# Relaid weights for a two-layer hybrid decoder step: each 1 MB slot read as 128 rows of 8 KB instead of 2 KB (and 4 KB) rows

## The chip, the cores and the metric

The kernel runs on one core of one Trainium2 chip. The metric is the device time of one execution in microseconds. Three runs of the kernel before took 2315.47, 2316.97 and 2317.2 us; the median is 2316.97 us. Host work (laying out arrays before the launch) is outside the metric.

## What is computed

The reference is one inference step of a decoder trunk with two layers, for 256 prompt tokens and 8 sequences of 8 tokens (320 tokens of width 1024, float32). Cut to the order of the work:

```python
for layer in range(2):
    mod = silu(c) @ w_ada[layer] + b_ada[layer]        # 1024 x 6144: six vectors of shift, scale and gate
    h = rmsnorm(x) * (1 + sc_m) + sh_m
    if layer == 0:
        out, states = mixer_ab(h)                      # h @ ab_w_in (1024 x 4104), delta rule + HGRN2, @ ab_w_out (1024 x 1024)
    else:
        out, states = mixer_ssd(h)                     # h @ ssd_w_in (1024 x 5152), SSD scan, @ ssd_w_out (2048 x 1024)
    x = x + g_m * out
    h = rmsnorm(x) * (1 + sc_f) + sh_f
    x = x + g_f * moe(h)                               # 16 experts, top 2 of one group; gate, up 1024 x 512, down 512 x 1024
y = rmsnorm(x)
```

All weights together are some 300 MB and each is read once from HBM in an execution.

## The kernel before

One core holds all 320 tokens in SBUF, with features on the 128 partitions. The weights stream through a ring of eight **slots** (`SLOTS = 8`), each 128 partitions x 2048 float32, that is 1 MB or 8 KB per partition. `load` (line 361) fills the next slot: SP waits until TensorE has counted `weights_used` far enough, then issues one DMA. TensorE takes slots in the same order with `next_slot` (line 561) and gives them back through `weights_used`.

What SP issues stands in program order and sets the order of the transfers: `load_cond` for blocks of `w_ada` (two slots for 512 columns), `load_square` for a matrix in blocks of 512 columns (one slot is 512 rows, so four rows of 2 KB per partition), and `experts` for the mixture of experts (MoE): per expert two slots each of gate, up (2 KB rows) and down (two rows of 4 KB per partition). The slot's source is a rearranged view of the weight as the caller gave it:

```python
wk = w.rearrange("(k p) n -> p k n", p=P)
for c0 in cols:
    for k0 in range(0, nk, 4):
        load(wk[:, k0:k0 + 4, c0:c0 + BANK])
```

At the start SP issues the conditioning vector `cs` (from `c_t`), two slots of `w_ada`, the tables `const` and `small`, then six slots more, `x`, and three small tails (`router`, `ab_tail`, `dt_tail`). TensorE's first wait is for `const` and `small` (line 1047).

In the MoE of each layer the tokens go through HBM. GpSimd scatters token rows of 4 KB into `x_rows` by ten indirect DMAs (line 490); SP loads 128 rows per expert from there (`tokens`, line 400); ACT stores each expert's result into `y_rows` (line 1315, 512 KB in rows of 4 KB); when all have landed, GpSimd gathers two rows per token from `y_rows` by ten indirect DMAs (line 497), and VectorE adds them into `x`. SP goes on meanwhile: after the last expert come the `w_ada` slots of `COND_BACK` and the next layer's first weights. These loads go out as TensorE frees slots.

The two output projections (`projections`, line 579) take all slots of a group of 512 columns before their first matmul: two for layer 0, four for `ssd_w_out` of layer 1. SP issues them after `mixer_done`.

DMAs go out on three queues: SP's (all weight loads and the `x_rows` loads), ACT's (the `y_rows` stores) and GpSimd's (the states in and out, the scatter, the gather and the final `y`). `y` is stored as 1024 rows of 320 values (line 537).

Of the kernel before, what the change touches and what calls it, by code (L numbers as in the profile page):

```python
# [25 lines left out]
P = 128  # L26
D = 1024
DK = D // P
PROMPT = 256
SEQS, SEQ_LEN = 8, 8  # L30
T = PROMPT + SEQS * SEQ_LEN
# [3 lines left out]
MODS = 1 + SEQS  # L35
TAPS = 4
PAD = TAPS - 1
# [4 lines left out]
HEADS = 4  # L42
BLOCKS = HEADS * CHUNKS
AB_CONV = 12
AB_TAIL = 2 * HEADS
AB_TAIL_AT = 2048

SX = 16
SG = 4
SHPG = 8  # L50
SH = SG * SHPG
SXBC = 24
SSD_IN = 5152
# [6 lines left out]
SLOT = 2048  # L60
SLOTS = 8
BANKS = 4
BANK = 512
# [6 lines left out]
COND_MIXED = ([(0, 8), (0, 9)], [(1, 8), (1, 9)])  # L70
# [72 lines left out]
def trunk_program(nc, a, out):  # L143
    with ExitStack() as ctx:
        def sb(name, cols, parts=P):
            return ctx.enter_context(nc.sbuf_tensor(name, [parts, cols], F32))

        def sem(name):
            return ctx.enter_context(nc.semaphore(name))
# [4 lines left out]
        x = sb("x", DK * T)  # L154
        h = sb("h", DK * T)
        cs = sb("cs", DK * MODS)
        mod0 = sb("mod0", 48 * MODS)
        router = sb("router", DK * E)
        ab_tail = sb("ab_tail", DK * AB_TAIL)
        dt_tail = sb("dt_tail", DK * SH)  # L160
# [34 lines left out]
        def slot(n):  # L195
            at = RING + (n % SLOTS) * SLOT
            return pool[:, at:at + SLOT]
# [40 lines left out]
        k = Plan((0, ab_free), (ab_lo_end, pool_cols))  # L238
# [52 lines left out]
        o = Plan((0, MOD1_AT - 2100))  # L291
# [9 lines left out]
        cond_in = sem("cond_in")  # L301
        x_in = sem("x_in")
        tails_in = sem("tails_in")
# [5 lines left out]
        weights_in = [sem(f"weights_in{i}") for i in range(SLOTS)]  # L309
# [37 lines left out]
        left_weights_in = by_layer("left_weights_in")  # L347
# [10 lines left out]
        @block.sync  # L358
        def _(sp):
            n = Count()  # L360

            def load(src):

                i = n.n.get(id(weights_used), 0)
                if i >= SLOTS:
                    sp.wait_ge(weights_used, n.at(weights_used, 1 - SLOTS))
                n.up(weights_used)
                sp.dma_start(slot(i).rearrange("p (k n) -> p k n", n=src.shape[-1]), src) \
                    .then_inc(weights_in[i % SLOTS], 16)

            def load_cond(groups):
                for layer, g_ in groups:
                    load_square(a["w_ada"][layer], [g_ * BANK], DK)

            def load_square(w, cols, nk):

                wk = w.rearrange("(k p) n -> p k n", p=P)
                for c0 in cols:
                    for k0 in range(0, nk, 4):
                        load(wk[:, k0:k0 + 4, c0:c0 + BANK])  # L380

            def experts(layer):
                wg, wu, wd = a["moe_w_gate"][layer], a["moe_w_up"][layer], a["moe_w_down"][layer]

                def gate_up(e):
                    for w in (wg, wu):
                        wk = w[bass.ds(e, 1)].rearrange("o (k p) n -> p (o k) n", p=P)
                        for k0 in (0, 4):
                            load(wk[:, k0:k0 + 4, :])

                def down(e):
                    wk = wd[bass.ds(e, 1)].rearrange("o (k p) n -> p (o k) n", p=P)
                    for k0 in (0, 2):
                        load(wk[:, k0:k0 + 2, :])

                def tokens(e, b, reuse=True):
                    if reuse:
                        n.up(xe_turned)
                        sp.wait_ge(xe_turned, n.at(xe_turned))
                    sp.dma_start(XE[b], x_rows[bass.ds(e * CAP, CAP), :]).then_inc(xe_in[b], 16)  # L400

                load_cond(COND_AGAIN[layer] + COND_ROUTE[layer] + COND_MOVE[layer])
                gate_up(0)
                sp.wait_ge(scattered, 16 * 2 * CHUNKS * (layer + 1))
                tokens(0, 0, False)
                tokens(1, 1, False)
                gate_up(1)
                down(0)
                with sp.Fori(0, TURNS) as i:
                    with n.repeat(i, TURNS, {weights_used: 6 * EXPERTS_A_TURN, xe_turned: EXPERTS_A_TURN}):  # L410
                        for j in range(EXPERTS_A_TURN):
                            e = i * EXPERTS_A_TURN + (2 + j)
                            tokens(e, j % 2)
                            gate_up(e)
                            down(i * EXPERTS_A_TURN + (1 + j))
                for e in range(2 + TURNS * EXPERTS_A_TURN, E):
                    tokens(e, e % 2)
                    gate_up(e)
                    down(e - 1)
                down(E - 1)  # L420
                n.up(xe_turned, 2)
                load_cond(COND_BACK[layer])
                sp.wait_ge(overflow_known, layer + 1)
                with sp.If(sp.value_load(overflow[0:1, layer:layer + 1], min_val=0, max_val=1) > 0):
                    with sp.Fori(0, E) as e:

                        sp.wait_ge(left_weights_free[layer], e + 1)
                        for i, w in enumerate((wg, wg, wu, wu, wd, wd)):
                            wk = w[bass.ds(e, 1)].rearrange("o (k p) n -> p (o k) n", p=P)
                            nk = wk.shape[1] // 2  # L430
                            sp.dma_start(slot(i).rearrange("p (k n) -> p k n", k=nk), wk[:, i % 2 * nk:(i % 2 + 1) * nk, :]) \
                                .then_inc(left_weights_in[layer], 16)
                    sp.wait_ge(left_weights_free[layer], E + 1)

            sp.dma_start(cs[:, :].rearrange("p (k n) -> p k n", k=DK), a["c_t"].rearrange("(k p) n -> p k n", p=P)).then_inc(cond_in, 16)
            load_cond(COND_FIRST[0][:1])
            for dst, src in ((const, a["consts"]), (small, a["small"])):
                sp.dma_start(dst[:, :], src).then_inc(consts_in, 16)
            load_cond(COND_FIRST[0][1:])
            sp.dma_start(x[:, :].rearrange("p (k n) -> p k n", k=DK), a["x_t"].rearrange("(k p) n -> p k n", p=P)).then_inc(x_in, 16)  # L440
            for dst, src, k_ in ((router, a["router_w"], DK), (ab_tail, a["ab_w_in"][0][:, AB_TAIL_AT:AB_TAIL_AT + AB_TAIL], DK),
                                 (dt_tail, a["ssd_w_in"][0][:, SSD_IN - SH:SSD_IN], DK)):
                sp.dma_start(dst[:, :].rearrange("p (k n) -> p k n", k=k_), src.rearrange("(k p) n -> p k n", p=P)).then_inc(tails_in, 16)
            load_cond(COND_NORM[0])
            load_square(a["ab_w_in"][0], [0, 512, 1024, 1536] + [AB_TAIL_AT + AB_TAIL + BANK * i for i in range(4)], DK)
            for layer, w_out, nk in ((0, a["ab_w_out"][0], DK), (1, a["ssd_w_out"][0], SX)):
                if layer == 1:
                    load_cond(COND_NORM[1])
                    load_square(a["ssd_w_in"][0], [BANK * i for i in range(4, 10)] + [BANK * i for i in range(4)], DK)

                sp.wait_ge(ring_opens, layer + 1)
                if layer == 0:
                    load_cond(COND_MIXED[0][:1])
                    load_square(a["w_ada"][0][0:BANK], [COND_MIXED[0][1][1] * BANK], DK // 2)
                    sp.wait_ge(mixer_done, 1)
                    load_square(a["w_ada"][0][BANK:D], [COND_MIXED[0][1][1] * BANK], DK // 2)
                else:
                    load_cond(COND_MIXED[1])
                    sp.wait_ge(mixer_done, 2)
                load_square(w_out, (0, BANK), nk)  # L460
                experts(layer)


# [1 line left out]
        def _(pool_eng):  # L465
            n = Count()

            def store(dst, src):

                pool_eng.wait_ge(out_ready, n.up(out_ready))  # L470
                n.up(stored, 16)
                pool_eng.dma_start(dst, src).then_inc(stored, 16)
# [61 lines left out]
                               SSS[q % 2].rearrange("p (b n) -> p b n", b=SEQS)).then_inc(stored_state[q % 2], 16)  # L534
            store(out["ssd_p"], ST)
            exchange(1)
            store(out["y"].rearrange("(k p) n -> p k n", p=P), h[:, :].rearrange("p (k n) -> p k n", k=DK))
            pool_eng.wait_ge(stored, n.at(stored))
            for i in range(2):
                pool_eng.wait_ge(stored_state[i], 16 * SG // 2)  # L540
# [1493 lines left out]

_WEIGHTS = ("w_ada", "ab_w_in", "ab_w_out", "ssd_w_in", "ssd_w_out", "moe_w_gate", "moe_w_up", "moe_w_down")


def _constants():  # L2040
# [100 lines left out]
```

## Time and profile before

| | |
|---|---|
| median of 3 runs | 2316.97 us (2315.47 to 2317.2) |
| profiled execution, span from first to last instruction | 2319.4 us (no other time is given for it) |
| PE busy | 1974.0 us, 85% |
| DVE, ACT, POOL busy | 600.3, 302.9, 53.9 us |
| mean granted TensorE clock | 0.827 |
| SP's queue (weights, x_rows) | 145776 packets, 321.13 MB |
| GpSimd's queue | 11632 packets, 50.98 MB |
| ACT's queue (y_rows stores) | 4608 packets, 16.78 MB |

The profile is of one execution on the chip; its times are microseconds from the first instruction. PE stands for TensorE's matmuls, PEld for its weight loads, DVE for VectorE, ACT for ScalarE, POOL for GpSimd, and a name with q (SPq, POOLq) for that engine's instruction queue. L944 is line 944 of the kernel. DMA transfers are read from the issue to the landing, and from the stretches of time in which the profile gives the gigabytes per second and the busy share of the 16 DMA engines (overlapping packets can take it a little over 1).

### The profile page before, as it was taken

To read this page: it belongs to the slowest core of one execution; us is meant where nothing else is said; L and a number is where in the kernel's file an instruction comes from. 1 tells how busy PE (TensorE), PEld (TensorE's weight loads), DVE (VectorE), ACT (ScalarE), POOL (GpSimd) and SP (SyncE) were. 2 spreads that over 40 slices of the span, in tenths; PEclk is the share of its full clock that TensorE was granted. 3 is DMA by queue.
4 is the path that set the end of the run, shared out by engine and by line. 5 is a ranking of instruction groups with operands and counts; after the bars stand their busy time and mean duration, and the time that the engine had idled before them with its cause. 6 is when DMAs were issued, how large, how long until landed. Compare 5 with 4: busy or idle time off the path is not lost.

```text
span 2319.4 us, 19065 instructions
## 1 busy us (share of the span) xinstructions
PE 1974.0 (85%) x7290; PEld 1146.4 (49%) x7290; DVE 600.3 (26%) x1226; ACT 302.9 (13%) x538; POOL 53.9 (2%) x68
## 2 busy tenths in 40 slices
PE   7999578758889999999689989999979599999972
PEld 2566378757453444444246655556636344444431
DVE  0230533374230000000234214575620300000004
ACT  1121201021011111111012210110000111111110
POOL 0000000000001000000100000000000100000001
PEclk9999655565889999999889985555589799999995
DMA  9880100010838888888823220220074188888842
GB/s 333 244 244 1 45 1 1 5 73 5 290 109 298 291 301 309 289 311 291 245 87 132 79 69 4 73 73 36 15 257 145 56 310 308 287 308 298 296 151 56
DMA packets 162097, 390.01 MB, mean 168 GB/s; under 512 B 10848, under 2 KB 12000, under 8 KB 161376
## 3 DMA queue, kind: packets, MB, share of 16 engines
q1 hardware_dynamic: 145776, 321.13, 40.7%
q0 software_dynamic: 11632, 50.98, 6.4%
q10 hardware_dynamic: 4608, 16.78, 1.8%
q8 instruction: 56, 0.92, 0.2%
q14 instruction: 25, 0.20, 0.0%
HBM read 339.87 MB, written 48.99 MB: 168 GB/s over the span
## 4 chain that ended last, share of the span: by engine, by line
PE 77%; DVE 9%; issue 6%; ACT 3%; DMA 3%; POOL 1%; DVEq 0%; SPq 0%; ACTq 0%; POOLq 0%
PE bank L944 29%; PE bank L587 18%; PE bank L657 5%; PE bank L612 4%; PE bank L892 2%; PE bank L897 2%; PE bank L868 2%; PE bank L887 1%; PE bank L636 1%; PE bank L730 1%; PE bank L884 1%; PE bank L628 1%; PE bank L697 1%; PE bank L936 1%; ACT pool L1296 1%
## 5 line engine op out<-in xcount | busy, mean ns | idle before, releaser
L944 PE MATMUL bank<-pool 128*128 128x512 f32 x1536 | 684.1, 598 | 35.1 <-PE bank L944 12.3
L944 PEld LDWEIGHTS bank<-pool 128*128 128x128 f32 x1536 | 285.6, 191 | 391.9 <-issue 385.8
L587 PE MATMUL bank<-h,pool 128*128 128x320 f32 x1280 | 354.2, 438 | 5.2 <-PE bank L587 5.2
L587 PEld LDWEIGHTS bank<-h,pool 128*128 128x128 f32 x1280 | 244.4, 192 | 113.6 <-issue 16.7
L612 PE MATMUL bank<-pool,cs 128*9 128x512 f32 x384 | 175.9, 612 | 14.3 <-DMA small<-small_in 12.0
L1935 DVE COPY pool<-bank 128x512 f32<-128x512 f32 x32 | 22.1, 691 | 506.1 <-PE bank L966 506.1
L657 PE MATMUL bank<-pool 64*64 64x64 f32 (+2 forms) x920 | 118.0, 327 | 22.2 <-DVE pool L1582 16.9
L657 PEld LDWEIGHTS bank<-pool 64*64 64x64 f32 (+2 forms) x920 | 114.7, 238 | 27.6 <-DVE pool L1582 18.3
L612 PEld LDWEIGHTS bank<-pool,cs 128*9 128x9 f32 x384 | 33.9, 93 | 145.1 <-issue 132.5
L1941 DVE TENSOR_TENSOR pool<-bank,pool 128x512 f32<-128x512 f32 x32 | 22.1, 691 | 244.7 <-PE bank L944 244.7
L587 PE MATMUL bank<-pool 128*128 128x320 f32 x256 | 71.3, 441 | 8.0 <-DMA pool<-ssd_w_out_in 7.6
L1296 ACT ACTIVATE pool<-bank 128x512 f32<-128x512 f32 x64 | 34.8, 594 | 274.1 <-PE bank L936 274.1
L892 PEld LDWEIGHTS bank<-pool 128*128 128x128 f32 x256 | 55.8, 330 | 23.7 <-issue 23.7
L1313 ACT ACTIVATE pool<-bank 128x512 f32<-128x512 f32 x64 | 38.2, 597 | 220.2 <-PE bank L944 220.2
L936 PE MATMUL bank<-const,pool 128*128 128x128 f32 x256 | 35.1, 281 | 35.5 <-DMA pool<-x_rows 25.2
L587 PEld LDWEIGHTS bank<-pool 128*128 128x128 f32 x256 | 49.5, 194 | 29.3 <-issue 9.9
L1465 DVE SCALAR_TENSOR_TENSOR pool<-pool,small 128x344 f32<-128x344 f32 x108 | 62.3, 576 | 3.8
L936 PEld LDWEIGHTS bank<-const,pool 128*128 128x128 f32 x256 | 28.1, 143 | 59.8 <-issue 34.4
L892 PE MATMUL bank<-pool 128*128 128x8 f32 x256 | 57.3, 362 | 0.0
L897 PE MATMUL bank<-pool 64*128 64x512 f32 x64 | 56.1, 1067 | 0.0
L628 PE MATMUL bank<-h,const 128*128 128x320 f32 x80 | 31.2, 559 | 27.3 <-ACT h L1098 25.2
L1303 ACT ACTIVATE pool<-bank 128x512 f32<-128x512 f32 x32 | 19.1, 598 | 230.9 <-PE bank L944 230.9
(334 smaller groups left out, 1526.7 us busy)
## 6 DMA issues: line engine op xcount, KB each, us to landing
pool<-moe_w_gate_in SPq DMA_DIRECT2D x64, 1024.0 KB, 7.7
pool<-moe_w_up_in SPq DMA_DIRECT2D x64, 1024.0 KB, 7.0
pool<-moe_w_down_in SPq DMA_DIRECT2D x64, 1024.0 KB, 5.1
pool<-w_ada_in SPq DMA_DIRECT2D x48, 1024.0 KB, 8.7
pool<-ssd_w_in_in SPq DMA_DIRECT2D x20, 1024.0 KB, 5.6
pool<-ab_w_in_in SPq DMA_DIRECT2D x16, 1024.0 KB, 12.1
pool<-x_rows SPq DMA_DIRECT2D x32, 512.0 KB, 5.7
y_rows<-pool ACTq DMA_DIRECT2D x32, 512.0 KB, 7.3
```

The source lines that it names most:

```text
L587: mm = pe.matmul(b[:, 0:T], ws[kk // 4][:, kk % 4, mt * P:(mt + 1) * P], rhs[:, kk * T:(kk + 1) * T], start=(kk == 0), stop=(kk == nk - 1))
L612: mm = pe.matmul(b[0:MODS, :], cs[:, (k0 + kk) * MODS:(k0 + kk + 1) * MODS], w[:, kk, :], start=(k0 + kk == 0), stop=(k0 + kk == DK - 1))
L628: mm = pe.matmul(b[:, 0:T], ones, h[:, kk * T:(kk + 1) * T], start=(kk == 0), stop=(kk == DK - 1))
L657: mm = pe.matmul(b[0:parts, (i - i0) * width:(i - i0 + 1) * width], lhs(i), rhs(i), start=True, stop=True)
L868: pe.matmul(b[0:C, 0:T], SEL[:, (gi * SHPG + hh) * C:(gi * SHPG + hh + 1) * C], G, start=True, stop=True).then_inc(dve_full, 1)
L892: mm = pe.matmul(reads[:, o:o + SEQ_LEN], states[:, s_ * BANK + j * P:s_ * BANK + (j + 1) * P], Cf[:, PROMPT + s_ * SEQ_LEN:PROMPT + (s_ + ...
L897: pe.matmul(b[:, :], BM[:, s_ * P:(s_ + 1) * P], XEND[:, PC * BANK:CHUNKS * BANK], start=True, stop=True).then_inc(dve_full, 1)
L936: mm = pe.transpose(b[:, (kk - k0) * P:(kk - k0 + 1) * P], XE[q][:, kk * P:(kk + 1) * P], ident)
L944: mm = pe.matmul(b[:, :], lhs[:, kk * CAP:(kk + 1) * CAP], ws[kk // per][:, kk % per, col:col + BANK], start=(kk == 0), stop=(kk == nk - 1))
L1296: act.activation(XT[q][:, i * BANK:(i + 1) * BANK], b[:, :], ACT.Copy).then_inc(act_free, 1)
L1313: act.activation(YE[q][:, i * BANK:(i + 1) * BANK], b[:, :], ACT.Copy).then_inc(act_free, 1)
L1465: ins = stt(cv, up[:, j:j + CVW], w[:, f * TAPS + j:f * TAPS + j + 1], cv, ALU.mult, ALU.add)
```

## The change

The host lays every large weight out in the order in which the slots are taken, so that the slot's bytes in HBM are 128 rows of 8 KB, one row per partition. `x`, `c`, `router`, the two tails and the output `y` are laid out by partition as well (`x` and `y` in rows of 10 KB). The bytes are the same, and no instruction of any engine is added, dropped or moved; each DMA keeps its place in its queue and loses its inner dimension.

```diff
-                sp.dma_start(slot(i).rearrange("p (k n) -> p k n", n=src.shape[-1]), src) \
-                    .then_inc(weights_in[i % SLOTS], 16)
+                sp.dma_start(slot(i), src).then_inc(weights_in[i % SLOTS], 16)
...
-                    load_square(a["w_ada"][layer], [g_ * BANK], DK)
+                    load_blocks(a["w_ada"][layer, g_])
...
+            def load_blocks(w):
+
+                for j in range(w.shape[0]):
+                    load(w[j])
...
+                def half(w, e, j):
+                    return w[bass.ds(e * 2 + j, 1)].rearrange("o p n -> (o p) n")
+
                 def gate_up(e):
                     for w in (wg, wu):
-                        wk = w[bass.ds(e, 1)].rearrange("o (k p) n -> p (o k) n", p=P)
-                        for k0 in (0, 4):
-                            load(wk[:, k0:k0 + 4, :])
+                        for j in range(2):
+                            load(half(w, e, j))
...
-            sp.dma_start(cs[:, :].rearrange("p (k n) -> p k n", k=DK), a["c_t"].rearrange("(k p) n -> p k n", p=P)).then_inc(cond_in, 16)
+            sp.dma_start(cs[:, :], a["c_t"]).then_inc(cond_in, 16)
...
-            store(out["y"].rearrange("(k p) n -> p k n", p=P), h[:, :].rearrange("p (k n) -> p k n", k=DK))
+            store(out["y"], h[:, :])
...
+def _rows(w):
+
+    w = np.asarray(w)
+    return w.reshape(-1, P, w.shape[-1]).transpose(1, 0, 2).reshape(P, -1)
...
+def _blocks(w, cols):
+
+    w = np.asarray(w)
+    return np.stack([w[:, c:c + BANK].reshape(-1, 4, P, BANK).transpose(0, 2, 1, 3).reshape(-1, P, SLOT) for c in cols])
...
+def _expert_halves(w):
+
+    layers, experts, rows, cols = w.shape
+    return w.reshape(layers, experts * 2, rows // (2 * P), P, cols).transpose(0, 1, 3, 2, 4).reshape(layers, experts * 2, P, SLOT)
```

The start of SP's program, before (the shape at a row's end is partitions x rows per partition x elements):

```order
L435 DMA cs<-c_t_in 128x8x9
L368 DMA pool<-w_ada_in 128x4x512 x2
L438 DMA const<-consts_in 128x1059
L438 DMA small<-small_in 128x438
L368 DMA pool<-w_ada_in 128x4x512 x6
L440 DMA x<-x_t_in 128x8x320
```

And the same place in the changed kernel:

```order
L435 DMA cs<-c_t_in 128x72
L368 DMA pool<-w_ada_in 128x2048 x2
L438 DMA const<-consts_in 128x1059
L438 DMA small<-small_in 128x438
L368 DMA pool<-w_ada_in 128x2048 x6
L440 DMA x<-x_t_in 128x2560
```

The order is the same; a slot's transfer has 128 rows where it had 512, `cs` has 128 rows of 288 bytes where it had 1024 of 36, and `const` and `small` are as they were.

## Rows read from the trace of the kernel before

**Rows 1.** The page: span, and TensorE's busy time, share and instructions.

```profile
span 2319.4 us, 19065 instructions
PE 1974.0 (85%) x7290; PEld 1146.4 (49%) x7290; DVE 600.3 (26%) x1226; ACT 302.9 (13%) x538; POOL 53.9 (2%) x68
```

**Rows 2.** Busy us by engine, PEclk, DMA share, GB/s: first MoE; last expert's end.

```profile
720.00:1105.00 385.00, 358.41 (x936) 158.77 (x936) 21.63 (x32) 45.39 (x78) 0.00 (x0) 1.00 0.85 301
...
2248.00:2252.00 4.00, 4.00 (x10) 1.52 (x8) 0.00 (x0) 0.60 (x1) 0.00 (x0) 1.00 0.00 0
```

**Rows 3.** Chain that ended last (start, us, what): one product mid-MoE, the last one.

```profile
885.90 7.12 PE bank L944 x16
...
2245.05 7.12 PE bank L944 x16
```

**Rows 4.** Waits for DMAs: total us, times, longest us.

```profile
PE bank L936 <- DMA pool<-x_rows: 25.2, 2, 23.9
...
PE bank L612 <- DMA small<-small_in: 12.0, 1, 12.0
...
PE bank L587 <- DMA pool<-ssd_w_out_in: 7.6, 1, 7.6
...
DVE pool L1962 <- DMA pool<-y_rows,pool: 35.7, 2, 27.1
```

**Rows 5.** Same columns as Rows 2: w_ada slots, 2 KB rows; gdn_state, 16 KB rows.

```profile
18.00:30.00 12.00, 11.70 (x31) 2.49 (x30) 0.20 (x1) 1.17 (x2) 0.00 (x0) 1.00 1.05 388
240.00:244.00 4.00, 0.88 (x8) 0.79 (x8) 2.83 (x9) 0.74 (x2) 0.00 (x0) 0.50 1.06 446
```

**Rows 6.** Timeline: first matmuls (start, us); columns of Rows 2: the stretch before.

```profile
11.99 9.55 PE L612 MATMUL bank<-pool,cs 128*9 128x512 f32 x16 [11.99 <-DMA small<-small_in]
...
3.50:12.00 8.50, 0.01 (x1) 0.01 (x1) 0.00 (x0) 0.21 (x1) 0.00 (x0) 1.00 1.03 385
```

**Rows 7.** DMA issues: KB each, median us from issue to landing.

```profile
y_out<-h POOLq DMA_DIRECT2D x1, 1280.0 KB, 5.3
ssd_p_out<-pool POOLq DMA_DIRECT2D x1, 1024.0 KB, 4.2
...
cs<-c_t_in SPq DMA_DIRECT2D x1, 36.0 KB, 2.7
```

**Rows 8.** Chain that ended last, before layer 1's output projection.

```profile
1704.47 11.80 DMA pool<-ssd_w_out_in
```

**Rows 9.** First scatter's last DMA (chain), and TensorE's wait behind it (timeline).

```profile
709.06 6.19 DMA x_rows<-pool
...
718.56 1.09 PE L936 MATMUL bank<-const,pool 128*128 128x128 f32 x8 [1.36 <-DMA pool<-x_rows]
```

**Rows 10.** Chain: last y_rows store and last gather of layer 0; last store, layer 1.

```profile
1113.57 7.39 DMA y_rows<-pool
...
1132.57 12.61 DMA pool<-y_rows,pool
...
2252.82 2.63 DMA y_rows<-pool
```

**Rows 11.** Columns of Rows 2: gather with loads, loads left over, gather alone.

```profile
1127.00:1144.00 17.00, 8.70 (x30) 2.33 (x28) 0.82 (x4) 1.18 (x2) 4.93 (x6) 0.88 1.04 243
...
1145.00:1150.50 5.50, 2.04 (x16) 1.86 (x16) 4.90 (x6) 0.00 (x0) 0.00 (x0) 0.50 1.03 382
...
2259.00:2270.00 11.00, 0.00 (x0) 0.00 (x0) 0.00 (x0) 0.00 (x0) 6.79 (x8) 0.50 0.92 207
```

**Rows 12.** hgrn_s_out's store (timeline; DMA issues), and its stretch beside w_ada loads.

```profile
580.53 0.53 POOL L472 DMA_DIRECT2D hgrn_s_out<-pool  x1 [19.59 <-DVEq L1393]
...
hgrn_s_out<-pool POOLq DMA_DIRECT2D x1, 2048.0 KB, 11.6
...
582.00:592.00 10.00, 6.67 (x34) 5.39 (x33) 2.51 (x4) 3.08 (x3) 0.00 (x0) 0.50 0.96 357
```

**Rows 13.** DMA issue (KB, us to landing) of the ssd_w_in slot issued at 1127.69.

```profile
pool<-ssd_w_in_in SPq DMA_DIRECT2D x1, 1024.0 KB, 18.8
```

More of the change, by code:

```diff
@@ L367, in load, with load_matrix @@
                 n.up(weights_used)
-                sp.dma_start(slot(i).rearrange("p (k n) -> p k n", n=src.shape[-1]), src) \
-                    .then_inc(weights_in[i % SLOTS], 16)
+                sp.dma_start(slot(i), src).then_inc(weights_in[i % SLOTS], 16)
             def load_cond(groups):
                 for layer, g_ in groups:
-                    load_square(a["w_ada"][layer], [g_ * BANK], DK)
[L375 to L380, printed above, removed]
+                    load_blocks(a["w_ada"][layer, g_])
+            def load_blocks(w):
+                for j in range(w.shape[0]):
+                    load(w[j])
+            def load_matrix(w):
+                for g_ in range(w.shape[0]):
+                    load_blocks(w[g_])
             def experts(layer):
                 wg, wu, wd = a["moe_w_gate"][layer], a["moe_w_up"][layer], a["moe_w_down"][layer]
+                def half(w, e, j):
+                    return w[bass.ds(e * 2 + j, 1)].rearrange("o p n -> (o p) n")
                 def gate_up(e):
                     for w in (wg, wu):
-                        wk = w[bass.ds(e, 1)].rearrange("o (k p) n -> p (o k) n", p=P)
-                        for k0 in (0, 4):
-                            load(wk[:, k0:k0 + 4, :])
+                        for j in range(2):
+                            load(half(w, e, j))
                 def down(e):
-                    wk = wd[bass.ds(e, 1)].rearrange("o (k p) n -> p (o k) n", p=P)
-                    for k0 in (0, 2):
-                        load(wk[:, k0:k0 + 2, :])
+                    for j in range(2):
+                        load(half(wd, e, j))
                 def tokens(e, b, reuse=True):
@@ L428, in experts @@
                         for i, w in enumerate((wg, wg, wu, wu, wd, wd)):
[L429 to L432, printed above, removed]
+                            sp.dma_start(slot(i), half(w, e, i % 2)).then_inc(left_weights_in[layer], 16)
                     sp.wait_ge(left_weights_free[layer], E + 1)
-            sp.dma_start(cs[:, :].rearrange("p (k n) -> p k n", k=DK), a["c_t"].rearrange("(k p) n -> p k n", p=P)).then_inc(cond_in, 16)
+            sp.dma_start(cs[:, :], a["c_t"]).then_inc(cond_in, 16)
             load_cond(COND_FIRST[0][:1])
@@ L439, in _ @@
             load_cond(COND_FIRST[0][1:])
[L440 to L443, printed above, removed]
+            sp.dma_start(x[:, :], a["x_t"]).then_inc(x_in, 16)
+            for dst, src in ((router, a["router_w"]), (ab_tail, a["ab_tail"]), (dt_tail, a["dt_tail"])):
+                sp.dma_start(dst[:, :], src).then_inc(tails_in, 16)
             load_cond(COND_NORM[0])
-            load_square(a["ab_w_in"][0], [0, 512, 1024, 1536] + [AB_TAIL_AT + AB_TAIL + BANK * i for i in range(4)], DK)
-            for layer, w_out, nk in ((0, a["ab_w_out"][0], DK), (1, a["ssd_w_out"][0], SX)):
+            load_matrix(a["ab_w_in"])
+            for layer, w_out in ((0, a["ab_w_out"]), (1, a["ssd_w_out"])):
                 if layer == 1:
                     load_cond(COND_NORM[1])
-                    load_square(a["ssd_w_in"][0], [BANK * i for i in range(4, 10)] + [BANK * i for i in range(4)], DK)
+                    load_matrix(a["ssd_w_in"])
                 sp.wait_ge(ring_opens, layer + 1)
@@ L453, in _ @@
                     load_cond(COND_MIXED[0][:1])
-                    load_square(a["w_ada"][0][0:BANK], [COND_MIXED[0][1][1] * BANK], DK // 2)
+                    last = a["w_ada"][0, COND_MIXED[0][1][1]]
+                    load(last[0])
                     sp.wait_ge(mixer_done, 1)
-                    load_square(a["w_ada"][0][BANK:D], [COND_MIXED[0][1][1] * BANK], DK // 2)
+                    load(last[1])
                 else:
@@ L459, in _ @@
                     sp.wait_ge(mixer_done, 2)
-                load_square(w_out, (0, BANK), nk)
+                load_matrix(w_out)
                 experts(layer)
@@ L2033, in _ @@
             normalise(None)
-_WEIGHTS = ("w_ada", "ab_w_in", "ab_w_out", "ssd_w_in", "ssd_w_out", "moe_w_gate", "moe_w_up", "moe_w_down")
+def _rows(w):
[7 more added lines that the diff above has]
+    return w.reshape(layers, experts * 2, rows // (2 * P), P, cols).transpose(0, 1, 3, 2, 4).reshape(layers, experts * 2, P, SLOT)
 def _constants():
@@ L2108 @@
         "consts": consts, "levels": levels, "small": _small(v),
-        "x_t": np.concatenate([v["x_prompt"].reshape(-1, D), v["x_sample"].reshape(-1, D)]).T,
-        "c_t": np.concatenate([v["c_prompt"], v["c_sample"]]).T,
-        "router_w": v["router_w"],
+        "x_t": _rows(np.concatenate([v["x_prompt"].reshape(-1, D), v["x_sample"].reshape(-1, D)]).T),
+        "c_t": _rows(np.concatenate([v["c_prompt"], v["c_sample"]]).T),
+        "router_w": _rows(v["router_w"]),
+        "ab_tail": _rows(v["ab_w_in"][0][:, AB_TAIL_AT:AB_TAIL_AT + AB_TAIL]),
+        "dt_tail": _rows(v["ssd_w_in"][0][:, SSD_IN - SH:SSD_IN]),
+        "w_ada": np.stack([_blocks(w, range(0, 6 * D, BANK)) for w in v["w_ada"]]),
+        "ab_w_in": _blocks(v["ab_w_in"][0], [BANK * i for i in range(4)] + [AB_TAIL_AT + AB_TAIL + BANK * i for i in range(4)]),
+        "ab_w_out": _blocks(v["ab_w_out"][0], (0, BANK)),
+        "ssd_w_in": _blocks(v["ssd_w_in"][0], [BANK * i for i in range(4, 10)] + [BANK * i for i in range(4)]),
+        "ssd_w_out": _blocks(v["ssd_w_out"][0], (0, BANK)),
+        "moe_w_gate": _expert_halves(v["moe_w_gate"]), "moe_w_up": _expert_halves(v["moe_w_up"]),
+        "moe_w_down": _expert_halves(v["moe_w_down"]),
         "gdn_conv_t": conv_t(v["state_gdn_conv"]), "ssd_conv_t": conv_t(v["state_ssd_conv"]),
@@ L2116 @@
     }
-    arrays |= {name: v[name] for name in _WEIGHTS}
     arrays = {name: np.ascontiguousarray(x) for name, x in arrays.items()}
-    shapes = {"y": (D, T), "gdn_p": (P, HEADS * P), "gdn_s": (P, SEQS * HEADS * P), "gdn_conv": (P, AB_CONV * MODS * PAD),
+    shapes = {"y": (P, DK * T), "gdn_p": (P, HEADS * P), "gdn_s": (P, SEQS * HEADS * P), "gdn_conv": (P, AB_CONV * MODS * PAD),
               "hgrn_p": (P, HEADS * P), "hgrn_s": (P, SEQS * HEADS * P), "ssd_p": (P, SH * C), "ssd_s": (P, SEQS, SH * C),
@@ L2132, in conv_out @@
         return m[:, 0:1], m[:, 1:]
-    y = r["y"].T
+    y = r["y"].reshape(P, DK, T).transpose(1, 0, 2).reshape(D, T).T
     gc, sc_ = conv_out(r["gdn_conv"]), conv_out(r["ssd_conv"])
```

## The prediction, made before the changed kernel ran

> **What bounds the kernel now.** Begin with the engines' busy times: TensorE is busy for 1974.0 of 2319.4 us, 85% [rows 1]. That is an average, so the stages come next. In the first MoE the matmuls take 358.41 of 385 us, at the full clock, while the DMA engines are busy for 0.85 of the time and move 301 GB/s [rows 2]. This is the stage with by far the most loads (192 of the 288 slots, six for each of 32 experts in both layers together), and its transfers hide behind TensorE. They do not slow the matmuls either: a product of 16 matmuls takes 7.12 us in the middle of it and 7.12 us at its end [rows 3], where almost nothing moves any more [rows 2]. So faster loads are worth nothing for two thirds of the slots.
>
> What can be gained stands in the waits for DMAs [rows 4]. TensorE waits 12.0 us at the start for `small`; 7.6 us for `ssd_w_out`; 25.2 us in two pieces for `x_rows`, of which 23.9 us lie in layer 1, where the scatter before it has no weight load beside it; and VectorE waits 35.7 us in two pieces for the gather from `y_rows`, 27.1 us of it at the end of layer 1, again with no weight load beside it. All other waits of TensorE are for other engines. The change therefore acts at five places: the start, the first scatter, the layer-0 gather, `ssd_w_out`, and the final store.
>
> **The price of a slot.** With 2 KB rows and a full queue the loads move 388 GB/s [rows 5], so a slot of 1.049 MB takes 2.70 us. No load of the trace has 8 KB rows. The nearest rows are the 16 KB rows of `gdn_state`: 446 GB/s over 4 us [rows 5], 2.35 us for a slot's bytes. Per engine of 16, a 2 KB row then costs 84.5 ns and a 16 KB row 588 ns, which a fixed 12.5 ns and 36.0 ns per KB fit; 8 KB would be 300 ns, or 2.40 us a slot. The 4 us stretch is short, so I take **2.45 us, 0.25 us saved per slot**, with 0 and 0.35 as ends.
>
> The Trainium skill, page "DMA: Bandwidth & Descriptors", section "Specifications", gives 512 bytes as the smallest transfer for line rate; by that, 2 KB rows are at line rate already, and the slots save nothing. The two stretches (388 against 446 GB/s) speak against it; what it would give is the second rival below.
>
> **The change part by part.** No instruction moves and no wait is added; the sum has these terms.
>
> 1. *Start.* `small` lands at 11.99 us, behind `cs` and two slots, on a queue that is full from 3.5 us on (385 GB/s) [rows 6]. Two slots save 0.5 us. `cs` took 2.7 us to land for 36 KB [rows 7]; before 3.5 us its 1024 short rows hold the queue. 128 rows instead save between 0 and 1 us; I take 0.4, nearer to 0, because most of 2.7 us is what any transfer takes (the last `y_rows` store, 512 KB, landed in 2.63 us [rows 10]). **-0.9** (ends 0 and -1.7). TensorE runs on without a DMA wait until the scatter, so this passes to the end. The larger early loads (`x`, the tails) become faster at no gain: TensorE is busy meanwhile.
>
> 2. *First scatter.* It runs beside two slots of the up weights, its last DMA takes 6.19 us, and TensorE waits 1.36 us for the load behind it [rows 9]. Two slots save 0.5 us of DMA time, of which I count **-0.3** (0 to -1.36, all that there is to gain).
>
> 3. *Layer-0 store and gather.* The last `y_rows` store takes 7.39 us where the undisturbed one of layer 1 takes 2.63, and the last gather 12.61 us [rows 10], because TensorE frees slots in these 30 us and SP refills them. Gather and loads together move only 243 GB/s with all DMA engines busy; the gather alone moves 207; after its end the loads go on at 382 GB/s for 5.5 us [rows 11]. So when the gather ended, 2.1 MB, two slots, were still to come. If long rows let the loads take a larger share, those two could at worst all run ahead of it: 2 x 2.45 = +4.9 us, less 4 x 0.25 for the slots that run ahead anyway: +3.9. At best the gather moves as if alone: its 2.62 MB (ten DMAs of 64 rows of 4 KB) at 207 GB/s take 12.7 us instead of 17: -4.3. Which end is nearer? The trace has one place where long rows meet short ones. `hgrn_s_out` is stored in 16 KB rows beside `w_ada` loads of 2 KB; it was issued at 580.53 and landed 11.6 us later, and from 582 to 592 us 3.57 MB moved in all [rows 12]. The store is 2.10 MB, so the loads got 1.47 MB, 0.70 byte per byte of the store, though their rows were an eighth as long. In the gather's 17 us, 4.13 MB moved, 1.51 of it loads: 0.58 per byte, with rows half as long. The share hardly follows the row length. I take a little of the bad end, **+0.7**.
>
> 4. *`ssd_w_out`.* Four slots are issued in a row and TensorE starts when the fourth lands, 11.80 us after its issue [rows 8]; the wait is 7.6 us [rows 4]. Four slots save **-1.0** (0 to -1.4). The other four are needed a whole projection group later and are hidden.
>
> 5. *Final store.* `y` (1280 KB in 1024 rows) lands in 5.3 us; `ssd_p_out`, 1024 KB in 8 KB rows, in 4.2 [rows 7]. A quarter MB more at 446 GB/s adds 0.6, so 4.8: **-0.5** (0 to -1.0).
>
> Elsewhere the loads have cover: the MoE's by the matmuls (0.15 of the DMA time free), the input projections' by TensorE's own pace, since no wait for them is listed. Cost 0 for these; if the cover went, see the last rival.
>
> Sum: -0.9 - 0.3 + 0.7 - 1.0 - 0.5 = **-2.0 us**, 0.09%. The profiled execution's span is 2.4 us above the median of the runs, 2316.97; I apply the difference to the median: **2315.0 us**. About 0.2%, 4.6 us, is what a measurement of this kernel can tell from no change, so the forecast is no difference.
>
> **Rivals.**
>
> *Long rows win over the gather (slower).* If an engine takes one row from each queue in turn, 8 KB of load goes for each 4 KB row of the gather and of the last store, the loads run first, and the gather lands up to 3.9 us later; with half of the other gains (-1.35) the kernel ends 2.5 us later: 2319.5. It decides from the point where the loads get more than about one byte per byte of the gather. For it: a slot issued in that stretch needs 18.8 us to land now [rows 13], so the loads are held back. Against it: the 0.70 above; strict turns would have left the loads 0.13. The Trainium skill, page "DMA: Bandwidth & Descriptors", section "Queues, rings and completion order", says that each engine goes round its queues packet by packet; by that rule this rival is the result. The stretch at 582 us does not bear it out in its strict form.
>
> *No gain in rate.* The slots stay at 2.70 us; what is left is `cs` and the final store, -0.9: 2316.1.
>
> *The gather is freed (faster).* If fewer, longer rows stop holding up the gather's, term 3 becomes -4.3, and the sum -7.0: 2310.0. For it: 243 GB/s with all engines busy is far under 388, so the mixture itself is what is slow. Against it: nothing shows that the number of rows is the cause, since the gather alone reaches only 207.
>
> *8 KB rows are slow (much slower).* An expert takes some 24.1 us (385 us for 16) and leaves 0.15 of DMA time free [rows 2], 0.60 us for each of its six slots. Above 3.3 us a slot (317 GB/s) the MoE waits for its weights; at 300 GB/s, 3.5 us, that is 0.2 x 192 = 38 us: 2355. Against it: 446 GB/s with 16 KB rows.
>
> **How the numbers follow.** Forecast 0.52, long rows win 0.20, no gain in rate 0.10, gather freed 0.13, slow rows 0.05. Faster by over 0.2% takes the freed gather and the forecast's best edge (0.08, where terms 1, 2, 4 and 5 near their best ends, -5.5): 0.21. Slower takes the slow rows, and 0.06 for long rows winning with none of the gains and the store late as well: 0.11. The rest, 0.68, is within. The range goes from the freed gather, 2310, to the long rows with none of the other gains (+3.9), 2320.9; it leaves out the slow rows and the tails.
>
> **What would show it.** In the changed profile: full-queue stretches of weight loads near 425 GB/s (right) or 388 (wrong); `small` landing near 11.1; the wait for `ssd_w_out` near 6.6 us; `y` landing in 4.8; SP's packets down by about 100,000; MoE products still 7.12 us. Term 3 is judged by the gather's last landing, counted from the last expert's store: now 31.6 us (1113.57 to 1145.18). Clearly more, and the long rows win; near 27, and it is freed. A MoE with waits for weights would make the prediction wrong altogether.

## The result and the profile after

The changed kernel takes **2324.14 us** (median of 12 runs, 2317.69 to 2329.88). The kernel before, timed beside it on the same chip, takes 2317.52 (12 runs, 2315.47 to 2321.93). The ratio is 1.0025, 95% interval 1.0013 to 1.0036: slower by 3.0 to 8.3 us, where 2 us faster was forecast; the median also lies above the upper end of the forecast range, 2320.9. The profiled execution of the change took 2329.88 us, its slowest run, with a span of 2328.1, 8.7 above the span of [rows 1].

First the page and the stretches that answer to [rows 1, 2, 5, 6]. Columns of the windows: stretch, length, busy us of PE, PEld, DVE, ACT and POOL, PEclk, DMA share, GB/s.

```profile
span 2328.1 us, 19065 instructions
PE 1971.3 (85%) x7290; PEld 1142.6 (49%) x7290; DVE 600.4 (26%) x1226; ACT 303.2 (13%) x538; POOL 53.6 (2%) x68
...
q1 hardware_dynamic: 47088, 321.13, 37.6%
```

```profile
18.00:30.00 12.00, 11.70 (x32) 2.46 (x30) 0.19 (x1) 1.17 (x2) 0.00 (x0) 1.00 1.02 415
3.50:12.00 8.50, 0.80 (x1) 0.11 (x2) 0.00 (x0) 0.00 (x0) 0.00 (x0) 1.00 1.02 417
720.00:1105.00 385.00, 358.85 (x935) 158.79 (x933) 21.42 (x31) 45.36 (x78) 0.00 (x0) 0.99 0.82 300
```

SP's queue (q1: packets, MB, share) moves the same 321.13 MB in 47088 packets; before it needed 145776. A full queue of loads runs at 415 to 417 GB/s where it ran at 385 to 388, so a slot takes 2.5 us and not 2.7. In the MoE the DMA share falls from 0.85 to 0.82, the rate stays, and TensorE's busy time is what it was: the faster loads buy nothing there.

Now the chain that ended last (start, us, what), the rows that answer to [rows 3, 8 to 10], and VectorE's and TensorE's waits (total us, times, longest) that answer to [rows 4].

```profile
708.10 7.44 DMA x_rows<-pool
...
1107.36 7.12 PE bank L944 x16
1115.13 7.61 DMA y_rows<-pool
1134.36 20.72 DMA pool<-y_rows,pool
1177.39 7.53 PE bank L628 x16
...
1200.35 4.78 PE bank L636 x80
1205.13 17.44 PE bank L587 x64
1222.86 17.48 PE bank L587 x64
...
1712.85 11.01 DMA pool<-ssd_w_out_in
```

```profile
DVE pool L1962 <- DMA pool<-y_rows,pool: 44.0, 2, 27.1
...
PE bank L936 <- DMA pool<-x_rows: 26.7, 2, 24.2
...
PE bank L587 <- DMA pool<-ssd_w_out_in: 6.5, 1, 6.5
```

The start, the first scatter's wait and the final store, that answer to [rows 6, 9, 7], in the timeline and in the DMA issues (KB each, us to landing):

```profile
11.20 1.02 PE L612 MATMUL bank<-pool,cs 128*9 128x512 f32 x1 [11.20 <-DMA small<-small_in]
...
718.85 1.70 PE L936 MATMUL bank<-const,pool 128*128 128x128 f32 x8 [2.57 <-DMA pool<-x_rows]
```

```profile
y_out<-h POOLq DMA_DIRECT2D x1, 1280.0 KB, 4.7
...
cs<-c_t_in SPq DMA_DIRECT2D x1, 36.0 KB, 1.8
```

Three of the five places became faster: `small` lands at 11.20 (11.99 before), `ssd_w_out` takes 11.01 us (11.80), `y` lands in 4.7 (5.3). The main loss stands in one row: the last gather of layer 0 takes 20.72 us where it took 12.61. From the issue of the last expert's store to the end of the gather it is now 1115.13 to 1155.08, **39.95 us, 8.35 more than before**. The store's own row hardly changes (7.39 to 7.61 us). VectorE's wait grows by the same 8.3, 35.7 to 44.0, and all of it in layer 0: the longest piece, layer 1's, is still 27.1.

What did the loads do in that time? The view of the DMA queues shows it. Each row is a queue with its packets, MB and share of 16 engines; q1 carries the loads, q0 the gather. First the kernel before from 1130 to 1144 us, then the change from 1130 to 1150.

```profile
q0 software_dynamic: 637, 2.10, 61.4%
q1 hardware_dynamic: 716, 1.43, 42.6%
```

```profile
q1 hardware_dynamic: 504, 3.74, 69.5%
q0 software_dynamic: 515, 1.68, 31.9%
```

Count rows, not bytes. (A queue's packets include some under 512 bytes, so the rows are counted from the megabytes.) Before, 2.10 MB of 4 KB gather rows are 513 rows, and 1.43 MB of 2 KB load rows are 698: 1.36 load rows for each gather row, 0.68 byte per byte. After, 1.68 MB are 410 gather rows and 3.74 MB are 456 load rows of 8 KB: 1.11 rows for each, but **2.2 bytes per byte**. The number of load rows that slip in between two gather rows hardly changed; each of them is four times as long. A gather row now comes every 0.78 us on each engine (20 us over 410/16 rows), before every 0.44 us (14 us over 513/16).

The loads run ahead of the gather, and at its end none is left:

```profile
1135.00:1154.00 19.00, 2.56 (x13) 0.82 (x10) 0.39 (x2) 0.59 (x1) 0.26 (x1) 0.61 0.94 252
1154.00:1158.00 4.00, 0.73 (x7) 0.73 (x8) 2.71 (x3) 0.00 (x0) 0.00 (x0) 0.50 0.00 0
```

Before, 5.5 us of loads at 382 GB/s followed the gather [rows 11], beside work that didn't need them. The same bytes now stand in front of it: from the last store's issue to the gather's end the loads' queue moved 6.06 MB before (1113.57 to 1145.18 us) and 8.06 MB in the change (1115.13 to 1155.08), two slots more.

```profile
q1 hardware_dynamic: 3049, 6.06, 63.2%
...
q1 hardware_dynamic: 1112, 8.06, 64.9%
```

### The profile page after: what moved, and what is told of

Its sections match the earlier page's. It is cut to its first block, busy times and chain, and to the rows that moved or that the text cites. A ratio compares the mean times of both kernels' runs of the same rounds, so it can differ in the third digit from the quotient of the medians.

```text
span 2328.1 us, 19065 instructions
## 1 busy us (share of the span) xinstructions
PE 1971.3 (85%) x7290; PEld 1142.6 (49%) x7290; DVE 600.4 (26%) x1226; ACT 303.2 (13%) x538; POOL 53.6 (2%) x68
## 3 DMA queue, kind: packets, MB, share of 16 engines
q1 hardware_dynamic: 47088, 321.13, 37.6%
## 4 chain that ended last, share of the span: by engine, by line
PE 77%; DVE 9%; issue 6%; DMA 3%; ACT 3%; POOL 1%; DVEq 0%; SPq 0%; ACTq 0%; POOLq 0%
PE bank L944 29%; PE bank L587 18%; PE bank L657 5%; PE bank L612 4%; PE bank L892 2%; PE bank L897 2%; PE bank L868 2%; PE bank L887 1%; PE bank L884 1%; PE bank L730 1%; PE bank L636 1%; PE bank L628 1%; PE bank L936 1%; PE bank L697 1%; DMA pool<-y_rows,pool 1%
## 5 line engine op out<-in xcount | busy, mean ns | idle before, releaser
L587 PE MATMUL bank<-h,pool 128*128 128x320 f32 x1280 | 351.3, 435 | 5.3 <-PE bank L587 5.3
L587 PEld LDWEIGHTS bank<-h,pool 128*128 128x128 f32 x1280 | 242.7, 191 | 112.6 <-issue 14.9
L612 PE MATMUL bank<-pool,cs 128*9 128x512 f32 x384 | 175.7, 612 | 13.5 <-DMA small<-small_in 11.2
L587 PE MATMUL bank<-pool 128*128 128x320 f32 x256 | 72.1, 445 | 6.9 <-DMA pool<-ssd_w_out_in 6.5
L1296 ACT ACTIVATE pool<-bank 128x512 f32<-128x512 f32 x64 | 34.9, 594 | 275.8 <-PE bank L936 275.8
L936 PE MATMUL bank<-const,pool 128*128 128x128 f32 x256 | 35.7, 285 | 37.0 <-DMA pool<-x_rows 26.7
L1313 ACT ACTIVATE pool<-bank 128x512 f32<-128x512 f32 x64 | 38.2, 597 | 220.4 <-PE bank L944 220.4
L587 PEld LDWEIGHTS bank<-pool 128*128 128x128 f32 x256 | 50.0, 196 | 28.6 <-issue 9.4
L1007 PE MATMUL bank<-const,pool 64*128 64x64 f32 x80 | 11.1, 317 | 51.7 <-DVEq L1393 47.7
```

Of the source, the lines that this page charges most:

```text
L587: mm = pe.matmul(b[:, 0:T], ws[kk // 4][:, kk % 4, mt * P:(mt + 1) * P], rhs[:, kk * T:(kk + 1) * T], start=(kk == 0), stop=(kk == nk - 1))
L612: mm = pe.matmul(b[0:MODS, :], cs[:, (k0 + kk) * MODS:(k0 + kk + 1) * MODS], w[:, kk, :], start=(k0 + kk == 0), stop=(k0 + kk == DK - 1))
L936: mm = pe.transpose(b[:, (kk - k0) * P:(kk - k0 + 1) * P], XE[q][:, kk * P:(kk + 1) * P], ident)
L1296: act.activation(XT[q][:, i * BANK:(i + 1) * BANK], b[:, :], ACT.Copy).then_inc(act_free, 1)
L1313: act.activation(YE[q][:, i * BANK:(i + 1) * BANK], b[:, :], ACT.Copy).then_inc(act_free, 1)
```

## The experiments

Two theories. **Turns**: at the gather each DMA engine gives the two queues about equally many rows in turn, so the length of the load rows sets the gather's pace. **Another cause**: a loss in some other place (first scatter, MoE), or one that comes from the weights being contiguous in HBM and not from the rows.

### Rows of 2 KB only at the gather

The changed kernel; the 24 slots that SP issues around the gather (four of `w_ada`, twenty of `ssd_w_in`) are still each one contiguous piece of HBM, but are read in 2 KB rows.

```diff
-                    load_cond(COND_NORM[1])
-                    load_matrix(a["ssd_w_in"])
+                    for g_ in range(2):
+                        load_short(a["w_ada_norm1"][g_])
+                    for g_ in range(10):
+                        load_short(a["ssd_w_in"][g_])
...
+    return np.stack([w[:, c:c + BANK].reshape(-1, 4, P, BANK) for c in cols])
```

> The changed kernel, with the 4 w_ada slots and the 20 ssd_w_in slots that SP issues around layer 0's gather laid out so that a slot is one piece of 1 MB in HBM but is read in rows of 2 KB. Theory (row length): gather as in the kernel before, last DMA about 12.6 us (20.7 in the changed kernel), time about 2 us under the kernel before, 2315 to 2317. Rival (that the slot is one piece of HBM, or anything else of the new layout, is the cause): 2322 to 2326, the gather's last DMA near 20 us.

Measured: 2315.40 us (11 runs) beside 2316.09 for the kernel before (20 runs), ratio 0.9994, 0.9983 to 1.0005. The chain of this kernel:

```profile
1112.97 7.10 DMA y_rows<-pool
1131.71 12.19 DMA pool<-y_rows,pool
```

The gather is back at 12.19 us, with contiguous weights. So the row length did it. What is left of the change is -3.9 to +1.2 us, which holds the -2.7 that the prediction's terms give without its third, but zero as well.

### Rows of 8 KB only at the gather

The converse: the kernel before, with only those 24 slots in 8 KB rows.

```diff
-                    load_cond(COND_NORM[1])
-                    load_square(a["ssd_w_in"][0], [BANK * i for i in range(4, 10)] + [BANK * i for i in range(4)], DK)
+                    for w in [a["w_ada_norm1"][g_] for g_ in range(2)] + [a["ssd_w_in_long"][g_] for g_ in range(10)]:
+                        for j in range(2):
+                            load(w[j])
```

> The kernel before, with only those 24 slots in rows of 8 KB. Theory: the gather's last DMA near 20 us, time 5 to 9 us above the kernel before, 2322 to 2327. Rival (the loss is elsewhere, as at the first scatter): within 2 us of the kernel before.

Measured: 2326.25 us (5 runs) beside the same 2316.09, ratio 1.0039, 1.0026 to 1.0053: **6 to 12 us slower**. Its chain:

```profile
1113.47 8.45 DMA y_rows<-pool
1133.54 19.49 DMA pool<-y_rows,pool
```

These 24 slots alone bring the whole loss, and none of the gains. The queues from 1130 to 1150 us:

```profile
q1 hardware_dynamic: 478, 3.41, 63.2%
q0 software_dynamic: 587, 1.93, 38.4%
```

That is 416 load rows of 8 KB and 471 gather rows, 0.88 for each.

### Rows of 4 KB at the gather

The changed kernel with the same 24 slots in 4 KB rows, as long as the gather's own.

```diff
-    return np.stack([w[:, c:c + BANK].reshape(-1, 4, P, BANK) for c in cols])
+    return np.stack([w[:, c:c + BANK].reshape(-1, 2, 2, P, BANK).transpose(0, 1, 3, 2, 4).reshape(-1, 2, P, 2 * BANK) for c in cols])
```

> The changed kernel, with the 24 slots around layer 0's gather in rows of 4 KB (2 KB gave a last gather DMA of 12.2 us and 2315.4 us, 8 KB 20.7 and 2324.1). Theory (each DMA engine takes one row from the loads and one from the gather in turn): rows as long as the gather's give the loads about one byte per byte of the gather; last gather DMA near 16 us, time between the two, 2318 to 2321. Rival (the engines share by bytes, and only rows past some length do harm): as with 2 KB, last DMA under 13.5 us, 2314 to 2317.

Measured: 2321.48 us (12 runs) beside 2317.02 (18 runs), ratio 1.0013, 1.0004 to 1.0022. Its chain, and its queues from 1124 to 1146 us:

```profile
1112.17 5.81 DMA y_rows<-pool
1129.59 18.27 DMA pool<-y_rows,pool
```

```profile
q1 hardware_dynamic: 720, 2.77, 55.7%
q0 software_dynamic: 713, 2.34, 47.9%
```

2.77 MB are 676 load rows, 2.34 MB are 571 gather rows: 1.18 for each. From the last store's issue to the end of the gather it is 35.7 us, between the 31.6 and 39.95 of the two kernels. The order came out as forecast, with the gather longer (18.27 us for 16) and the time 0.5 us above the forecast's 2318 to 2321; the rival of that run, a last gather under 13.5 us, is out. The dose follows the length of the rows:

| load rows | load rows per gather row | bytes per byte | one gather row per engine | last gather DMA |
|---|---|---|---|---|
| none (8 KB rows with the wait, below) | 0 | 0 | 0.32 us | 4.9 us |
| 2 KB (before) | 1.36 | 0.68 | 0.44 us | 12.61 us |
| 2 KB only at the gather | 1.45 | 0.73 | 0.46 us | 12.19 us |
| 4 KB | 1.18 | 1.2 | 0.62 us | 18.27 us |
| 8 KB only at the gather | 0.88 | 1.8 | 0.68 us | 19.49 us |
| 8 KB (the change) | 1.11 | 2.2 | 0.78 us | 20.72 us |

Each row is counted in a stretch of 12 to 22 us of that kernel's gather (1128 to 1143 us for the third, with 1.54 MB of loads and 2.12 MB of gather). By the second and fourth columns a load row of 2 KB adds (0.44 - 0.32)/1.36 = 0.09 us to a gather row, one of 8 KB (0.78 - 0.32)/1.11 = 0.41, and (0.68 - 0.32)/0.88 = 0.41 where only the 24 slots have such rows. Alone on a full queue they take 0.084 us at 388 GB/s and 0.32 at 415. So a gather row pays at least the full price of every load row that goes in between.

### The loads wait for the gather

In both kernels, SP waits for the gather before it issues those 24 slots. The `w_ada` slots of `COND_BACK` stay ahead of the wait.

```diff
                 if layer == 1:
+                    sp.wait_ge(gathered, 16 * 2 * CHUNKS)
                     load_cond(COND_NORM[1])
```

With 8 KB rows:

> The changed kernel (8 KB rows everywhere), but SP waits for layer 0's gather to land before it issues the next layer's first loads (4 slots of w_ada, then ssd_w_in). Theory (8 KB rows of loads beside the gather hold its 4 KB rows back): the last y_rows store lands in about 3 us instead of 7.6, the gather in about 16 us from its first issue to its last landing (31.5 us in the changed kernel), and since TensorE has its own work until about 1138 us the kernel ends some 12 us or more under the changed one and under the kernel before: 2305 to 2312. Rival (the loss lies in the first scatter and elsewhere, the gather's delay is covered): within 3 us of the changed kernel's 2324. Rival (ssd_w_in then comes too late): a new wait of TensorE for ssd_w_in of over 3 us.

With 2 KB rows:

> The kernel before (2 KB rows) with the same wait. Theory: the gather lands as in the run with 8 KB rows and the wait, about 16 us after its first issue, since the length of rows that aren't there can't matter; the time is 8 to 12 us under the kernel before, and 2 to 3 us above the run with 8 KB rows and the wait (start, ssd_w_out and final store; less what the first scatter loses with long rows). Rival (the gather's rate depends on something other than the loads beside it): the gather stays above 20 us.

Measured: 2310.35 us with 8 KB rows (10 runs, ratio 0.9976, 0.9966 to 0.9985), 2307.55 with 2 KB rows (5 runs, 0.9959, 0.9946 to 0.9973), both beside 2316.09. With 8 KB rows, the timeline of ACT's, GpSimd's and SP's issues, and the gather's queue from 1116 to 1128 us:

```profile
1111.19 0.35 ACTq L1316 DMA_DIRECT2D y_rows<-pool  x1
...
1114.65 0.92 POOL L498 DMA_INDIRECT pool<-y_rows,pool  x1 [408.71 <-DMA y_rows<-pool]
...
1130.39 1.99 SPq L368 DMA_DIRECT2D pool<-w_ada_in  x4
```

```profile
q0 software_dynamic: 734, 2.43, 89.9%
```

and two windows of the same kernel (columns as above):

```profile
1116.00:1128.00 12.00, 11.40 (x31) 2.47 (x30) 0.43 (x2) 1.17 (x2) 7.90 (x9) 1.00 0.90 202
...
1132.00:1140.00 8.00, 3.46 (x26) 2.14 (x24) 5.63 (x8) 0.59 (x1) 0.00 (x0) 0.83 0.99 409
```

The store lands in time for the gather to be issued 3.5 us after it (8.4 in the change: 1115.13 to 1123.55), the gather ends 15.7 us after its first issue, and SP's loads start behind it, 19.2 us after the store's issue where the change needed 39.95. TensorE ends its own work for `COND_BACK` at 1133.98, in the chain `1133.56 0.42 PE bank L602 x4`, and is then the later of the two. SP has room for this: the held slots move at 409 GB/s, and neither kernel lists a wait for `ssd_w_in`. So the loads that ran beside the gather were never urgent, in the kernel before either.

The loss of the long rows is gone with the transfers that ran into each other. Between the two kernels with the wait there are 2.8 us, to the disadvantage of the long rows, where 2 to 3 us to their advantage had been forecast; the intervals overlap. The next runs bear on that gap.

### Long rows in the rest, short ones in the MoE

The kernel with the wait and 8 KB rows, but the MoE's slots read in rows of 2 KB (gate, up) and 4 KB (down). It asks whether the long rows cost something in the MoE.

```diff
-                    return w[bass.ds(e * 2 + j, 1)].rearrange("o p n -> (o p) n")
+                    return w[bass.ds(e * 2 + j, 1)].rearrange("o k p n -> p (o k) n")
...
-    return w.reshape(layers, experts * 2, rows // (2 * P), P, cols).transpose(0, 1, 3, 2, 4).reshape(layers, experts * 2, P, SLOT)
+    return w.reshape(layers, experts * 2, rows // (2 * P), P, cols)
```

> 8 KB rows and the wait for the gather, but the MoE's slots in rows of 2 KB (gate, up) and 4 KB (down), from one piece of HBM each. If long rows cost time at the scatter or inside the MoE: 2305 to 2308, under the run with the wait and 8 KB rows everywhere (2310.4). If that run's time has another cause: 2309 to 2311.

Measured: 2309.27 us (6 runs) beside 2317.02, ratio 0.9956, 0.9943 to 0.9970. With the 0.9976 (0.9966 to 0.9985) of the kernel with 8 KB rows throughout, on another chip, the intervals overlap: no cost of the long rows in the MoE is shown. The median fits the forecast for another cause (2309 to 2311), not the one for a cost (2305 to 2308).

### The first scatter held free as well

Both waits together: the loads around the gather as above, and of expert 0's slots only the gate's go out before the scatter; the up slots come behind the first load of tokens.

```diff
-                gate_up(0)
+                gate_up(0, (wg,))
                 sp.wait_ge(scattered, 16 * 2 * CHUNKS * (layer + 1))
                 tokens(0, 0, False)
+                gate_up(0, (wu,))
                 tokens(1, 1, False)
```

> 8 KB rows, the wait for the gather, and the first expert's two up slots moved behind the first token load, so that no weight load runs beside the scatter either. Theory (8 KB loads beside the scatter cost about 2 to 3 us, which is why the run with the wait took 2310.4 us with 8 KB rows and 2307.6 with 2 KB): TensorE's wait for x_rows in layer 0 falls from 3.7 us to about 2, time 2306 to 2308. Rival (something else in the run with 8 KB rows costs it): 2309 to 2311.

> The same two waits with 2 KB rows. Theory: no transfer that TensorE waits for has weight loads beside it any more, so row length counts only by the rate: 2 to 3 us above the run with 8 KB rows and the same waits. Rival (long rows cost time inside the MoE): 1 to 3 us below it.

Measured beside 2317.02: **2302.54 us with 8 KB rows** (6 runs, 2295.97 to 2307.15, ratio 0.9932, 0.9917 to 0.9947), 2306.98 with 2 KB rows (7 runs, 0.9953, 0.9935 to 0.9971). TensorE's wait for the scattered tokens with 8 KB rows:

```profile
PE bank L938 <- DMA pool<-x_rows: 23.8, 1, 23.8
```

It has one piece where it had two: layer 0's is gone, layer 1's stays. The version with both waits and 8 KB rows is 14.5 us (12.3 to 19.2) below the kernel before, and below the changed kernel too, which wasn't timed beside it. That is also below the 2306 to 2308 forecast, so the wait at the scatter doesn't account for all of it: beside the kernel before, the second wait added 8.7 us with 8 KB rows (5.7 to 14.5) and 1.5 with 2 KB rows (8.5 to 10.0), where the waits of TensorE that went away are 3.7 and 3.3 us. These are comparisons between chips, with runs of one kernel up to 14.3 us apart. Here the long rows are ahead by 4.4 us, with one wait they were behind by 2.8, on different chips, and in both pairs the intervals overlap. So what the long rows give once the gather is out of their way isn't settled; the forecast's -2.7 lies between.

## Why the prediction was wrong, by its own steps

- **The price of a slot** was right in kind: 2.5 us measured (415 to 417 GB/s), 2.45 taken, 2.70 before. The Trainium skill's rule in the page "DMA: Bandwidth & Descriptors", section "Specifications", that 512 bytes suffice for line rate would have left 388 GB/s; the rows decide against it.
- **Term 1, start:** -0.9 forecast, -0.8 measured (11.99 to 11.20; `cs` lands in 1.8 us where it took 2.7). Right.
- **Term 2, first scatter:** -0.3 forecast, +1.2 measured in the profiled pair (wait 1.36 to 2.57 us). It isn't shown to be the rows: the scatter's last DMA took 7.44, 6.20, 5.28 and 4.98 us in four profiles with up slots of 8 KB rows beside it and 6.19, 6.43, 5.81 and 5.24 in four with 2 KB rows.
- **Term 3, store and gather:** +0.7 forecast, **+8.35 measured**. This is the step that failed, at two sentences. The first is "The share hardly follows the row length". It compared bytes at the store of `hgrn_s_out` and at the gather and found 0.70 and 0.58 alike. (The 0.58 counts all 2.62 MB of the gather into 17 us; the queue view has 2.38 MB of gather and 1.74 MB of loads there, 0.73.) The queue view of the store's stretch, 582 to 592 us, has the rows, first before, then in the change:

```profile
q0 software_dynamic: 144, 2.10, 49.0%
q1 hardware_dynamic: 736, 1.47, 46.8%
...
q1 hardware_dynamic: 232, 1.77, 50.8%
q0 software_dynamic: 128, 2.10, 48.9%
```

  Before, some 5.6 load rows (1.47 MB in 2 KB) go by for each 16 KB row of that store, and 1.36 for each row of the gather. In the change it is 1.7 rows of 8 KB at the store: 0.84 byte per byte where it was 0.70. So at the store the sentence holds, and the bytes stay while the rows drop; at the gather the rows stay and the bytes go from 0.68 to 2.2. The last `y_rows` store is like the other store: from its issue to its landing the loads move 1.98 MB before and 2.32 MB in the change, 7.6 and 2.2 rows for each of its 128 rows, and it takes 7.39 and 7.61 us. The two kinds of place share the DMA engines differently, so one could not price the other; equal bytes before were a coincidence. The stores write to HBM and the gather reads from it, as the loads do; that this is the reason wasn't tried. Read by rows, the gather's own stretch had the answer: 1.36 load rows for each gather row, so 8 KB rows make it 2.7 bytes per byte, and 2.2 came.
- The second is the bound of **+3.9**, two slots at full rate. It counted the load bytes that could still run ahead, and that count was right (8.06 against 6.06 MB). But in the mixture they don't run at 2.45 us a slot: from 1135 to 1154 us gather and loads together move 252 GB/s, and a slot's 1.05 MB at that rate takes 4.2 us. Two of them, +8.3, are what came.
- **Term 4, `ssd_w_out`:** -1.0 forecast; the chain's row went from 11.80 to 11.01 us, the wait from 7.6 to 6.5, -1.1. **Term 5:** -0.5 forecast, `y` 5.3 to 4.7 us, -0.6. Both right, and other profiles agree: with 8 KB rows `ssd_w_out` takes 10.95 to 11.07 us in five (12.31 in the kernel with both waits) and `y` 4.7 or 4.8 in all six, with 2 KB rows 11.80 to 11.87 and 5.3 in four. **Elsewhere 0**: the MoE's products still take 7.12 us and TensorE has no new wait for a DMA. In the profiled pair the time from the first expert's first matmul to the last store's issue still grew from 395.0 to 396.3 us; with 2 KB rows and the wait at the gather it was 395.9, so this isn't shown to be the rows.
- **The rival "Long rows win over the gather"** was the mechanism, with its own condition met: more than a byte of load per byte of gather (2.2). Its price was that bound, and the same stretch at 582 us was the evidence against it that kept its chance at 0.20. Of its two transfers only the gather lost; the last `y_rows` store did not. The Trainium skill's page "DMA: Bandwidth & Descriptors", section "Queues, rings and completion order", has the engine go round its queues in turn, a packet of several descriptors at a time; the gather's rows agree with turns of equally many rows, at 0.88 to 1.45 each, and the store's rows at 582 us, with 5.6 and 1.7, do not. These counts can't tell turns of single rows from turns of several.

The sum with the measured values in place: -0.8 + 8.35 - 1.1 - 0.6 = +5.9 us without the first scatter's +1.2, and +7.1 with it; the medians differ by 6.6. The profiled pair hides part of this and adds to it elsewhere: its offset is +9.9 at the product behind the gather (1167.48 to 1177.39), +6.4 a few groups later, and +8.7 in the end.

## What to carry to other kernels

Where a transfer of short rows that work waits for shares the DMA engines with prefetch, count in the queue view how many rows of the one go by for each row of the other: where that count stays, as at the gather here, lengthening the prefetch's rows lengthens every turn, whatever it does for the prefetch's own rate. A prefetch that nothing waits for is better held back until such a transfer has landed; that was worth more here than the layout, in both layouts. A share seen between a store and loads did not price one between a gather and loads.

## What the runs showed of the hardware

The gather alone reaches 202 GB/s (1116 to 1128 us with the wait), half of what loads with long rows reach, with the DMA engines busy for 0.90 of the time: a gather row of 4 KB comes every 0.32 us on each engine, as long as an 8 KB load row takes at 415 GB/s.

TensorE's granted clock after the gather differs from profile to profile. It is 0.50 (1.2 GHz) in both kernels in the 22 us behind the gather, in which TensorE is busy for 5.5 us (from 1145 us before, from 1155 in the change), and 1.00 (2.4 GHz) again in the products that follow. Then, at L636 and the first L587, it is 0.50 once more for some time in the kernel before, and not in the change; the two rows are of before and of the change. Why isn't shown.

```profile
1192.00:1200.00 8.00, 8.00 (x46) 6.57 (x45) 0.32 (x1) 0.00 (x0) 0.00 (x0) 0.50 0.07 25
```

```profile
1184.00:1232.00 48.00, 47.05 (x222) 27.11 (x221) 20.73 (x37) 8.00 (x21) 0.00 (x0) 1.00 0.36 131
```

The groups at L636 and the first at L587 take 4.78 + 17.44 us at the full clock and took 6.84 + 20.21 before, so the change got 4.8 us back there. This doesn't go with the row length: the first group took 17.44 us with 2 KB rows and the wait, 19.05 with 8 KB rows and the wait. The runs of one kernel on one chip lie several us apart (12.2 us over the 12 runs of the change); whether the clock is the cause isn't shown. So 2 us of gain could only be read from the rows of single waits, not from the medians.
